# Second block's input projections as Strassen pairs, with sums in two ring slots that the stage has used up

## The reference

```python
for l in range(DEPTH_2):                       # 2 layers; x: 512 tokens, ctx: 256 tokens, d = 1024
    hx = x * (1 + sc1) + sh1
    hc = ctx * (1 + mod_c[1]) + mod_c[0]
    qx, kx, vx, cbx, ccx, cvx, gux, gvx = jnp.split(hx @ w_in[l], SPLIT_POINTS, axis=-1)
    qx, kx = axial_rope(qx, row, col), axial_rope(kx, row, col)
    # last layer: of ctx only keys and values; else the same eight parts of hc @ w_in[l]
    att_x = window_attention(qx, kx, vx, kc, vc, attn_sink[l])
    o_x = concatenate([att_x, local_mixers(cbx, ccx, cvx, gux, gvx, ...)]) @ w_out[l]
    ...                                        # layer norm, routed experts, layer norm
```

## Time and profile before

| | us |
|---|---|
| median of 3 timed runs | 3042.11 |
| lowest, highest | 3040.23, 3042.42 |
| the profiled execution's own time | 3041.03 |
| its span in the trace | 3039.2 |
| PE busy in the span | 2687.7 (88%) |
| DVE, ACT, POOL busy | 1225.9, 652.6, 418.8 |

### The profile page before, as it was taken

How to read it: one execution, slowest core, us unless ns; L and a number is a source line. 1 busy time by engine, 2 the same in 40 slices (tenths; PEclk the granted TensorE clock), 3 DMA queues, 4 the chain that set the end, 5 groups by cost and what they waited for, 6 DMA issues and landing times. The chain is left out here.

```text
span 3039.2 us, 44944 instructions
## 1 busy us (share of the span) xinstructions
PE 2687.7 (88%) x17074; PEld 1738.8 (57%) x17075; DVE 1225.9 (40%) x2425; ACT 652.6 (21%) x1342; POOL 418.8 (14%) x465
## 2 busy tenths in 40 slices
PE   7999989999999998989958998999788984898755
PEld 5877766488884574557545454544444642454423
DVE  5752367249999912226161111111413623222114
ACT  3540178120000010127131000000221621010002
POOL 3432012015440000000001010000100001121101
PEclk9999899999999999989988999999899996899877
DMA  3231320237545632110028889999622025899994
GB/s 141 90 127 58 136 77 26 72 97 241 209 180 209 242 139 75 56 62 1 28 76 359 342 350 414 418 397 380 251 92 91 1 82 218 350 370 378 404 420 165
DMA packets 137319, 594.60 MB, mean 196 GB/s; under 512 B 20336, under 2 KB 40588, under 8 KB 90608
## 3 DMA queue, kind: packets, MB, share of 16 engines
q1 hardware_dynamic: 86704, 359.25, 31.2%
q10 hardware_dynamic: 41808, 212.75, 17.5%
q0 software_dynamic: 8688, 21.00, 1.9%
HBM read 574.06 MB, written 33.69 MB: 200 GB/s over the span
## 5 line engine op out<-in xcount | busy, mean ns | idle before, releaser
L1405 DVE SCALAR_TENSOR_TENSOR psum<-weight_ring,condition_rows 128x1024 f32<-128x1024 f32 x192 | 268.1, 1396 | 16.0 <-issue 0.9
L174 PE MATMUL psum<-modulated,weight_ring 128*128 128x384 f32 (+2 forms) x640 | 228.7, 518 | 0.0
L2825 DVE COPY expert_hidden_turned<-psum 128x128 f32<-128x128 f32 (+1 forms) x93 | 32.6, 351 | 460.7 <-PE psum L2683 460.7
L2672 PE MATMUL psum<-weight_ring,slot_rows_turned 128*32 128x256 f32 x2176 | 147.3, 417 | 74.7 <-DMA weight_ring<-in_w_dram 46.6
L2661 PE MATMUL psum<-weight_ring,slot_rows_turned 128*64 128x256 f32 x1792 | 205.6, 383 | 0.6 <-issue 0.6
L174 PEld LDWEIGHTS psum<-modulated,weight_ring 128*128 128x128 f32 x640 | 121.4, 190 | 105.5 <-issue 51.0
L2661 PEld LDWEIGHTS psum<-weight_ring,slot_rows_turned 128*64 128x64 f32 x1792 | 127.7, 138 | 76.1 <-issue 16.9
L2690 PE MATMUL psum<-weight_ring,expert_hidden_turned 128*32 128x256 f32 (+1 forms) x1536 | 168.0, 445 | 0.0
L2753 ACT ACTIVATE expert_silu<-psum 64x256 f32<-64x256 f32 (+1 forms) x91 | 34.6, 380 | 607.1 <-PE psum L2661 323.1
L2808 DVE COPY slot_rows_turned<-psum 128x256 f32<-128x256 f32 (+1 forms) x93 | 50.6, 544 | 281.1 <-PE psum L2637 280.8
L174 PE MATMUL psum<-ffn_hidden,weight_ring 128*128 128x512 f32 (+1 forms) x440 | 154.6, 514 | 4.1 <-DVE ffn_hidden L1450 4.1
(11 more groups left out here) (476 smaller groups left out, 4274.5 us busy)
## 6 DMA issues: line engine op xcount, KB each, us to landing
third_stream_weights<-in_w_dram ACTq DMA_DIRECT2D x93, 2048.0 KB, 14.6
weight_ring<-in_w_dram SPq DMA_DIRECT2D x84, 2048.0 KB, 16.6
weight_ring<-in_w_ada_dram SPq DMA_DIRECT2D x24, 2048.0 KB, 9.4
weight_ring<-in_w_ffn_dram SPq DMA_DIRECT2D x11, 2048.0 KB, 12.4
weight_ring<-in_w_rnn_dram SPq DMA_DIRECT2D x8, 1536.0 KB, 6.6
weight_ring<-in_w_att_dram SPq DMA_DIRECT2D x6, 2048.0 KB, 8.0
weight_ring<-in_w_in_dram SPq DMA_DIRECT2D x6, 2048.0 KB, 13.2
weight_ring<-in_w_down_dram SPq DMA_DIRECT2D x8, 1408.0 KB, 6.0
```

The lines of the kernel that those rows point to most:

```text
L174: last = nc.tensor.matmul(out, weights[:, k * P:(k + 1) * P], rhs(k), start=(k == 0), stop=(k == tiles - 1))
L1405: last = v.scalar_tensor_tensor(out=product, in0=w[:, t], scalar=1.0, in1=CR[:, n, :], op0=ALU.mult, op1=ALU.mult, accum_out=c.mod[:, i // ...
L2672: last = nc.tensor.matmul(ps[units.rows(2 * m + o), 2 + b, 0:256], XT[:, b, k % tiles, units.rows(k // tiles)], w[:, k, 256 * o:256 * (o + ...
L2825: v.tensor_copy(HT[:, b, :, :], ps[:, 1, 0:256].rearrange("p (k s) -> p k s", k=2)[:, :, 0:2 * cap])\
```

## The change

The twelve tiles 0 to 11 become six pairs, `PAIRS = (8, 10, 0, 2, 4, 6)`: the queries first, then cc, cx, cb, gu. The keys (tile 12) are projected plainly, straight after the values, and the gate matmuls follow them. `width` is half of the token columns: 384 in layer 0, 256 in layer 1. The sums T1, T2, T4 and the six weight sums lie in the ring slots of `w_nat2` and of the keys' chunk, once these have been read; T3 overwrites a quarter of `HX`. So the last use of these two slots is the last pair. The chunks of `w_in2` come in the order 12, 8 to 11, 0 to 3, 4 to 7. In the pair code, `tight` (one PSUM bank for the products six and four) adds two waits, and the wait for the token sums moves from before the first pair to behind its first product, in the first block too. VectorE's work is written out by hand in a new order between the pairs' sums.

```diff
@@ pair_products @@
-    if p >= 2:
-        f.whole_read.wait(pe, p - 1)
+    if p >= f.depth:
+        f.whole_read.wait(pe, p - f.depth + 1)
     product(f.bank1(p), top[:, 0:KH * P], B11, stops=False)
+    if p == 0:
+        f.token_sums.wait(pe, 1)
     f.weight_sums.wait(pe, 4 * p + 2)
+    if p >= 1 and f.tight:
+        f.crossed.wait(pe, p)
     product(f.bank6, f.S2(p), f.T2)
...
     product(f.bank1(p), top[:, KH * P:], B21, starts=False)
+    if f.tight:
+        f.diagonal.wait(pe, p + 1)
     product(f.bank4, bottom[:, KH * P:], f.T4)
@@ recurrent_mixer @@
-                f.token_sums.wait(pe, 1)
@@ second_chunks @@
-        out += [tiles("w_in2", 0, 4, 13), tiles("w_in2", 4, 4, 13), tiles("w_in2", 8, 4, 13), tiles("w_in2", 12, 1, 13)]
+        out += [tiles("w_in2", 12, 1, 13), tiles("w_in2", 8, 4, 13), tiles("w_in2", 0, 4, 13), tiles("w_in2", 4, 4, 13)]
@@ mixer_inputs @@
+        width = (S if last_layer else T) // 2
+        keys = whole + [(S, C)] if last_layer else whole
+        PAIRS = (8, 10, 0, 2, 4, 6)
+        f, each, nrot = c.pairs, KH * width, 5
+        at_nat, at_keys, at_in = ring.uses, ring.uses + 1, ring.uses + 2
+        slots, cursor = (ring.view(at_nat), ring.view(at_keys)), [0, 0]
...
+        T1, T2, T4 = (by_tile(piece(r, each)) for r in (0, 0, 1))
+        formed = [piece(0 if cursor[0] + KH * P <= Ring.WORDS else 1, KH * P) for n in range(6)]
...
+        f.place(c, width, (0,), (1, 2, 3, 1), (T1, T2, HX[:, 0:KH, width:2 * width], T4), formed, outer, inner)
...
+            @block.gpsimd
+            def _(pool):
+                nat_read.wait(pool, TT)
+                z_read.wait(pool, len(keys))
+                for p, tile in enumerate(PAIRS):
+                    weight_sums(c, pool, p, *in_pair(four(ring.take(pool, n=at_in + p // 2)), tile))
...
-                ring.used(nat_ready.sem, nat_ready.base + TT)
...
-                            ring.used(z_ready.sem, z_ready.base + u)
...
-                ring.used(z_ready.sem, z_ready.base + len(pieces))
...
+                z_read.wait(pe, len(keys))
+                for p, tile in enumerate(PAIRS):
+                    pair_products(c, pe, p, *in_pair(four(ring.take(pe, n=at_in + p // 2)), tile), HX)
+                    for m, j in (((0, 4),), ((1, 0), (2, 1)), ((3, 2), (4, 3)), (), (), ())[p]:
+                        rotate(m, j)
+                done = lambda n: (f.product.sem, f.product.base + 7 * n)
+                for i in range(3):
+                    ring.used(*done(2 * i + 2), n=at_in + i)
+                ring.used(*done(len(PAIRS)), n=at_nat)
+                ring.used(f.crossed.sem, f.crossed.base + len(PAIRS), n=at_keys)
...
+                f.crossed.wait(act, len(PAIRS))
+                nc.scalar.activation(CX[:, 0, width:2 * width], CX[:, 0, width:2 * width], ACT.Gelu_apprx_tanh)
+                nc.scalar.activation(CX[:, 1, 0:2 * width], CX[:, 1, 0:2 * width], ACT.Gelu_apprx_tanh)\
+                    .then_inc(z_read.sem, 1)
...
+                v.tensor_tensor(f.T1, B12, B11, ALU.subtract)
                 root_ready.wait(dve, 1)
...
+                v.tensor_tensor(f.T2, B22, f.T1, ALU.subtract)
+                z_read.wait(dve, len(keys))
+                v.tensor_tensor(f.T3, B22, B12, ALU.subtract)
+                dve.drain()
+                v.tensor_tensor(f.T4, f.T2, B21, ALU.subtract).then_inc(f.token_sums.sem, 1)
+                gm_ready.wait(dve, 1)
...
+                inner_of(0)
+                outer_of(0)
+                rotated(0, 4)
+                inner_of(1)
+                outer_of(1)
+                inner_of(2)
+                rotated(1, 0)
+                rotated(2, 1)
+                outer_of(2)
+                rotated(3, 2)
+                rotated(4, 3)
+                inner_of(3)
+                outer_of(3)
...
+                short_conv(0)
+                inner_of(4)
+                short_conv(1)
+                outer_of(4)
...
+                times(4)
+                inner_of(5)
+                outer_of(5)
+                z_read.wait(dve, len(keys) + 1)
+                times(6)
```

More of the change, by code:

```diff
@@ L1689, in place @@
                 for start, end in ((0, S), (S, T)):
-                    a, b = max(at, start), min(at + n, end)
+                    a, b = max(at, start), min(at + width, end)
                     if a < b:
@@ L1693, in place @@
                 return out
[L1694 to L1704, removed]
-        with nc.Block(no_gpsimd_drain=True) as block:
+            if tile in (2, 3, 6, 7):
+                return [(CX[:, tile % 2, at:at + width], 0, width)]
+            return [(MIX[:, tile if tile < 8 else tile - 8, at:at + width], 0, width)]
+        scale_of = lambda tile: HD ** -0.5 if tile >= 8 else 1.0
+        with nc.Block(no_gpsimd_drain=True) as block:
+            @block.gpsimd
[4 more added lines that the diff above has]
+                    weight_sums(c, pool, p, *in_pair(four(ring.take(pool, n=at_in + p // 2)), tile))
             @block.tensor
             def _(pe):
-                w = ring.take(pe, KT * NPIECE).rearrange("p (k n) -> p k n", k=KT)
+                ring.uses += 5
+                w = ring.take(pe, KT * NPIECE, n=at_nat).rearrange("p (k n) -> p k n", k=KT)
                 for i in range(TT):
@@ L1717, in _ @@
                     last.then_inc(nat_ready.sem, 1)
-                ring.used(nat_ready.sem, nat_ready.base + TT)
[L1720 to L1724, removed]
+                w = ring.take(pe, KT * P, n=at_keys)
+                for u, (at, n) in enumerate(keys):
+                    project(nc, ps[:, u, 0:n], w, lambda k: HX[:, k, at:at + n]).then_inc(z_ready.sem, 1)
+                v_ready.wait(pe, 1)
@@ new lines, in _ @@
+                nat_read.wait(pe, TT)
+                consts.wait(pe, 16 * 6)
+                for h in range(2):
+                    for i in range(ntok):
+                        for g in (2 * h, 2 * h + 1):
+                            bank, to = (4 + h, i * P) if i < ST else (6, h * C + (i - ST) * P)
+                            last = nc.tensor.matmul(ps[64 * (g % 2):64 * (g % 2) + 64, bank, to:to + P],
+                                                    VG[:, i, P + g * 64:P + (g + 1) * 64], WS[:, g, :],
+                                                    start=True, stop=True)
@@ L1725, in rotate @@
+                last.then_inc(gm_ready.sem, 1)
+                def rotate(m, j):
+                    if j < 4:
+                        f.whole_read.wait(pe, j // 2 + 1)
+                        f.crossed.wait(pe, j // 2 + 1)
+                    else:
+                        v_ready.wait(pe, 2)
+                    if m >= 2:
+                        rot_read.wait(pe, m - 1)
                     src = MIX[:, j, 0:S] if j < 4 else K[:, 0:S]
-                    nc.tensor.matmul(ps[:, 6 + j % 2, :], ROT[:, :], src, start=True, stop=True)\
+                    nc.tensor.matmul(ps[:, 6 + m % 2, :], ROT[:, :], src, start=True, stop=True)\
@@ L3224, in build_program @@
         c.pairs = Pairs(c)
+        early_pairs(c)
         with ExitStack() as first:
```

177 lines of the change are left out of this document (103 added, 74 removed).

## The result

| | before | after |
|---|---|---|
| median, us | 3042.11 (5 runs) | 3057.12 (5 runs) |
| lowest, highest | 3040.23, 3043.03 | 3053.96, 3060.29 |
| span of the profiled execution | 3039.2 | 3053.7 |
| PE busy | 2687.7 | 2657.9 |

The ratio of the times is 1.0052 [1.0038, 1.0066]. The forecast was 3061 us, from 3052 to 3071, slower. TensorE is busy for 29.8 us less, and the span of the profiled execution is 14.5 us longer.

What follows compares the result with a forecast made beforehand. TensorE was taken to bound the two stages, and the mask and sink on SP's queue the attention's start. 3041.03 + 8.0 + 12.6 - 1.0 = 3060.6, said as 3061 us; range 3052 to 3071 for 8 in 10.

Steps and rivals of the forecast that it cites:

- The main step: End of both stages: five 2048 KB chunks leave SP together ahead of the mask; attention starts 8.0 and 12.6 us later.
- The rival by which the mask isn't held up behind the chunks: Start of both attentions: the mask isn't delayed, the stages' gains stand, 3020 us, faster; chance 10%.
- half-hidden rival: SP's queue: mask overtakes some chunks or loads run twice as fast, landing 10 us sooner per layer; near 3041 us; 5%.
- in layer 0's stage: Layer 0: TensorE ends 13.5 us sooner, but VectorE is free for the attention at 1358.1 against 1350.06, 8.0 us later.
- in layer 1's stage: Layer 1: TensorE ends 8.9 us sooner, but VectorE is free for the attention at 2358.3 against 2345.74, 12.6 us later.
- The burst: End of each stage: five chunks and the mask take 29.4 us from the first issue, plus 0.3 for the sink.
- its estimate of 27.3 us: Loads at each stage's end: the skill's fit for 11.0 MB, which would take 4 us off the two layers together.
- The stall behind the first product: First pair in layer 0's stage: TensorE waits 2.0 us for token sums T3 and T4, 3.2 us each.
- The other reading: Layer 0's token sums: a fixed 0.9 us lost per operation, so T3 and T4 take 2.7 us each, stall near 1.0.
- No wait between the pairs: Later pairs in both stages: waits for VectorE's and GpSimd's sums are covered by matmuls and taken as nothing.
- The rival of a late VectorE: Both stages: VectorE's inserted work holds each pair by 1 us or more, loads 12 us later, 3073 us; chance 12%.
- First block: First pair of the first block: its first product fills TensorE's 1.19 us wait for token sums; gain 1.0 us (0 to 1.2).

Runs made afterwards that it cites:

- e1: The changed kernel with the stage's five ring loads issued from SP behind the attention's mask and sink instead of ahead of them; 3012.78 us, 0.9901 of before.
- e3: The changed kernel with two of the five ring loads ahead of the mask and three behind it and the sink; 3028.3 us, 0.9955 of before.
- e4: The changed kernel with the mask and the sink issued from ScalarE's queue, the five ring loads still on SP's; 3025.56 us, 0.9948 of before.
- e8: The kernel before with only the first block's wait for token sums moved behind the first pair's first product; 3039.28 us, 0.9995 of before.
- e2: The kernel before, plain projections, with the slot of the values' weights counted as used only when the last tile is done; 3076.58 us, 1.0117 of before.

## Why the prediction was right, point by point

**The main step held.** SP's queue, freed at the end of the stage, sends five chunks ahead of the mask, and VectorE starts the attention late. The rival by which the mask isn't held up behind the chunks falls with its 24.4 us in after. What it assumed, a mask that lands in 3.3 us, had to be made by an edit (e1), and the time was then 3013 us, below even the 3020 that this rival named. In the half-hidden rival the mask lands 10 us sooner in each layer; in after it doesn't, and e3 and e4 (14 to 16 us sooner, 3028 and 3026 us) had to change the order or the queue for it.

**The sizes, stage by stage.** The terms by the two profiled executions (each stage from the issue of its constants, each attention from VectorE's first instruction in it):

| | forecast | measured |
|---|---|---|
| up to layer 0's stage | -1.0 | +0.6 |
| in layer 0's stage | +8.0 | +6.4 |
| between the two, to layer 1's stage | 0 | -3.5 |
| in layer 1's stage | +12.6 | +13.0 |
| after layer 1's stage | 0 | -2.0 |
| sum | +19.6 | +14.5 |

The two stages alone give 19.4 us of the 20.6 forecast for them. That the time is as near as 4 us is in part luck: the first block's miss (+1.6) and layer 0's (-1.6) cancel, and the 5.5 us between and after the stages are in no term of the forecast.

*Layer 0's stage, 8.0 forecast, 6.4 measured.* The burst takes 29.0 us from the first issue to VectorE, not 29.7. (The fit of the Trainium skill from which the prediction had its estimate of 27.3 us, DMA: Bandwidth & Descriptors, "Anatomy of one DMA", is given for DMAs that GpSimd issues; here SP issues them.) The stall behind the first product is 1.0 us, not 2.0. GpSimd's and TensorE's timelines of after:

```profile
1211.97 2.78 POOL L247 TENSOR_TENSOR weight_ring<-weight_ring 128x512 f32<-128x512 f32 x1 [302.47 <-ACT keys L1830]
1214.91 2.59 POOL L249 TENSOR_TENSOR weight_ring<-weight_ring 128x512 f32<-128x512 f32 x1 [0.16 <-issue]
...
1214.02 2.85 PE L262 MATMUL psum<-modulated,weight_ring 128*128 128x384 f32 x8
1217.64 2.82 PE L262 MATMUL psum<-weight_ring 128*128 128x384 f32 x8 [0.78 <-POOL weight_ring L249]
```

The first product ends at about 1216.6 (eight records at 0.646 us a pair), and the second starts at 1217.64. The name of the stall was wrong too: T4 is done at 1216.37, before the first product ends, and TensorE waits for GpSimd's second weight sum, until 1217.50. The forecast took 3.2 us for each token sum by proportion; T3 took 1.76, not slowed at all, and T4 2.67, longer by 0.9. The other reading, given beside it (a fixed loss of 0.9 us an operation), holds for T4 and not for T3, and its 1.0 us for the stall is right by luck, since the token sums alone leave no stall. T3 had started 0.1 us before GpSimd, and GpSimd's sum took 2.78 instead of 1.25; T4 started while GpSimd was at work, and lost 0.9. The Trainium skill (SBUF — State Buffer, "SBUF: two separate sides") has the shared ports as an exclusive lock that whoever starts first holds for a whole instruction; the trace agrees, 1.76, 2.78 and 2.67 us in this order.

*Layer 1's stage, 12.6 and 13.0.* TensorE's part took 91.1 us against 90.2 forecast, and the burst 29.1 against 29.7. The stall for GpSimd was 1.6 us, counted as in layer 0 from the end of the first product, against 1.5 forecast for the token sums.

*No wait between the pairs.* Besides these two, the list of TensorE's waits has none on VectorE's or GpSimd's sums in either stage; VectorE is busy 56 of 127 us. The rival of a late VectorE falls.

*First block, -1.0.* This term failed: up to layer 0's stage it is +0.6. The product does fill the wait. After starts it at 36.30 where the earlier trace rows has 37.37, and e8 shows the same gain by the next load. What it gains is lost again by 345 us, where the granted clock was 0.95 instead of 0.98 in after and e8. The early product doesn't bring that about by itself: e4 has it and keeps 0.98, e2 lacks it and shows 0.93. Over the kernels with it `cmp_probs` went out between 342.1 and 347.3 us, over those without between 345.1 and 348.6, both spreads wider than the gain. Single profiles can't tell a term of 1 us here, and what sets the clock stays open.

*Between and after the stages, -3.5 and -2.0.* No step of the forecast had this, and it is most of the difference between +19.6 and +14.5 us. The attention and what follows it up to layer 1's stage, in stretches, first of before and then of after: the attention with the first half of the output projection, the router, the experts. The 43 us of the output projection's second half are left out.

```profile
1350.06:1479.74 129.68, 122.44 (x807) 89.25 (x808) 65.13 (x152) 71.82 (x176) 4.58 (x28) 0.94 0.00 1
...
1522.30:1614.41 92.11, 52.98 (x308) 39.34 (x310) 54.77 (x163) 33.28 (x52) 6.02 (x7) 0.76 0.27 98
1614.41:2211.60 597.19, 532.48 (x3714) 298.82 (x3710) 100.62 (x208) 68.54 (x122) 58.81 (x87) 0.95 0.92 368
```

```profile
1356.99:1484.99 128.00, 119.44 (x807) 87.23 (x808) 65.10 (x152) 71.72 (x176) 4.59 (x28) 0.96 0.00 1
...
1527.90:1618.90 91.00, 52.28 (x308) 39.00 (x310) 54.88 (x163) 31.68 (x50) 6.02 (x7) 0.76 0.26 96
1618.90:2215.07 596.17, 531.32 (x3714) 298.58 (x3710) 100.62 (x208) 70.15 (x124) 58.40 (x87) 0.95 0.92 369
```

It is the same work, record for record (807, 308, 3714), and TensorE takes 3.0 us less for the first stretch's 807, at a clock of 0.96 instead of 0.94. Likewise behind layer 1: 68.42 us busy become 66.98 in the router's stretch, and 366.92 become 365.12 in the experts'. In e2, the other kernel with a long wait ahead of the attention, layer 0's first stretch takes 128.0 us at 0.96 as well; in e1, without that wait, it takes 127.99 at 0.96 too, and in e4, with pairs and a wait of 11.65 us, 129.73 at 0.94. So neither the wait nor the pairs decide it. Over all the kernels here the way from the attention's start to layer 1's stage takes 858.1 to 861.7 us, and the way from the start of layer 1's attention to the end 691.5 to 695.9 us; e2, a plain kernel, has 858.5 and 693.8, and e4, with pairs, 861.5 and 692.6. So these 5.5 us can't be put down to the change, and what sets the clock here stays open.

## What to carry to other kernels

A shorter stage pays only if its follower can start: look at what the follower's first load stands behind in its queue, not only at what its engines wait for now. Scratch space in ring slots moves their release to the end of the stage, and all loads that used to go out beside the work then go out in one burst. Small loads that gate a stage belong ahead of such a burst, or on another queue. The first of these turned 0.5% slower into 1.0% faster here, while by itself, without the pairs, it was worth nothing that could be told.

## What the hardware showed that I had not expected

- The issue itself stalls behind a burst: the 4 KB sink took SP 2.13 us to issue behind five chunks and the mask, and 0.43 us in e1 ahead of them and in e3 behind two.
- A second queue does not bring the mask back to 3.3 us: ScalarE's queue gave 8.7, and 10.8 for the 4 KB sink behind it, which then was what VectorE waited for.
- Before alone spread over 3032.14 to 3045.92 us in 23 runs of one job. Of a change worth 1 us nothing can be told from so few runs as here.
